# The up projection of a feed-forward as seven products of half blocks, with the weight sums on GpSimd

## The reference

```
h   = h + gate1 * (mixed @ w_out)
hn  = rms_norm(h, norm2_g) * (1 + scale2) + shift2
u   = depthwise_conv_centred(hn @ w_up, conv_w, conv_b)   # w_up: 1024 x 5632, 3 taps along tokens
val, gate = split(u)                                      # 2816 columns each
h   = h + gate2 * ((silu(gate) * val) @ w_down)
```

## Time and profile before

| | |
|---|---|
| median of 3 runs | 1614.38 us (1614.13 to 1614.63) |
| the profiled execution's own time | 1614.99 us |
| its span in the trace | 1613.1 us |
| TensorE busy | 1248.3 us (77%) |
| VectorE busy | 403.0 us (25%) |
| ScalarE busy | 228.1 us (14%) |
| GpSimd busy | 51.8 us (3%) |
| up projection (first to last product) | 228.5 to 384.6 us |

### The profile page before, as it was taken

How to read it: one execution, slowest core, us unless ns; L and a number is a source line. 1 busy time by engine, 2 the same in 40 slices (tenths; PEclk the granted TensorE clock), 3 DMA queues, 4 the chain that set the end, 5 groups by cost and what they waited for, 6 DMA issues and landing times.

```text
span 1613.1 us, 16506 instructions
## 1 busy us (share of the span) xinstructions
PE 1248.3 (77%) x7090; PEld 689.2 (43%) x7090; DVE 403.0 (25%) x817; ACT 228.1 (14%) x447; POOL 51.8 (3%) x77
## 2 busy tenths in 40 slices
PE   7999999999999999998665575666665556565556
PEld 4776578888888889852111111111111111111111
DVE  4667744454033557430000000000000000000001
ACT  2324622222103231120000000000000000000001
POOL 1100000000000031000000000000000000000000
PEclk9999999999999999998887878887888887888788
DMA  9987878667644435589999999999999999999997
GB/s 374 223 230 290 327 255 277 224 235 254 247 150 153 133 108 209 202 341 429 429 428 428 428 428 427 428 428 429 428 429 429 429 428 428 428 428 428 428 428 293
DMA packets 110881, 545.21 MB, mean 338 GB/s; under 512 B 5884, under 2 KB 73468, under 8 KB 80092
## 3 DMA queue, kind: packets, MB, share of 16 engines
q1 hardware_dynamic: 105068, 521.69, 81.6%
q0 software_dynamic: 3328, 18.43, 3.0%
q10 hardware_dynamic: 2416, 4.07, 0.7%
HBM read 539.97 MB, written 4.19 MB: 337 GB/s over the span
## 4 chain that ended last, share of the span: by engine, by line
PE 48%; DMA 41%; DVE 5%; another core or an unknown queue 4%; ACT 1%; issue 1%; SPq 1%; DVEq 0%; ACTq 0%
DMA arena<-in_exp_w_dram 21%; PE L L1658 12%; DMA ring<-in_exp_w_dram 9%; DMA tok<-in_exp_w_dram 9%; PE L L1897 7%; PE X L2116 6%; PE L L1846 5%; PE X L2144 3%; PE X L1824 3%; PE L L2016 2%; PE L L1788 2%; DMA ring<-in_w_ada_dram 2%; PE L L2157 1%; PE X L1946 1%
## 5 line engine op out<-in xcount | busy, mean ns | idle before, releaser
L2116 PE MATMUL X<-arena,side 128*32 128x512 f32 x1280 | 195.4, 741 | 125.3 <-DMA arena<-in_exp_w_dram 125.3
L1658 PE MATMUL L<-tok,ring 128*128 128x256 f32 x960 | 210.1, 380 | 1.2 <-ACT tok L632 0.7
L1658 PEld LDWEIGHTS L<-tok,ring 128*128 128x128 f32 x960 | 181.6, 190 | 32.9 <-issue 8.8
L2116 PEld LDWEIGHTS X<-arena,side 128*32 128x32 f32 x1280 | 39.4, 122 | 272.4 <-DMA arena<-in_exp_w_dram 199.6
L1492 DVE TENSOR_TENSOR side<-side,X 128x512 f32<-128x512 f32 x16 | 11.0, 687 | 502.7 <-ACT side L901 502.7
L2116 PE MATMUL X<-ring,side 128*32 128x512 f32 x512 | 84.3, 790 | 66.7 <-DMA ring<-in_exp_w_dram 66.7
L2144 PE MATMUL X<-ring,side 128*32 128x512 f32 x512 | 82.7, 783 | 27.7 <-DMA ring<-in_exp_w_dram 20.8
L1897 PE MATMUL L<-tok,ring 128*128 128x256 f32 x448 | 99.4, 379 | 0.3 <-ACT tok L753 0.3
L1897 PEld LDWEIGHTS L<-tok,ring 128*128 128x128 f32 x448 | 84.3, 190 | 13.9 <-issue 3.1
L901 ACT ACTIVATE side<-X 128x512 f32<-128x512 f32 x16 | 9.6, 597 | 519.2 <-PE X L2116 519.2
L1497 DVE TENSOR_TENSOR side<-X,side 128x512 f32<-128x512 f32 x16 | 11.1, 691 | 279.1 <-PE X L2144 279.1
(11 more groups left out here) (380 smaller groups left out, 1314.9 us busy)
## 6 DMA issues: line engine op xcount, KB each, us to landing
arena<-in_exp_w_dram SPq DMA_DIRECT2D x96, 2048.0 KB, 50.1
ring<-in_exp_w_dram SPq DMA_DIRECT2D x64, 2048.0 KB, 50.1
ring<-in_w_in_dram SPq DMA_DIRECT2D x34, 1024.0 KB, 5.6
more<-in_exp_w_dram SPq DMA_DIRECT2D x15, 2048.0 KB, 49.5
tok<-in_exp_w_dram SPq DMA_DIRECT2D x15, 2048.0 KB, 49.8
ring<-in_w_ada_dram SPq DMA_DIRECT2D x24, 1024.0 KB, 8.8
ring<-in_w_up_dram SPq DMA_DIRECT2D x22, 1024.0 KB, 7.7
arena<-in_ada_w_dram POOLq DMA_DIRECT2D x15, 1024.0 KB, 7.1
```

The source lines that it names most:

```text
L1658: last = MM(L[:, j % 4, m * T:m * T + T], w[:, k, m * P:m * P + P], src(k), start=(k == 0), stop=(k == KT - 1))
L2116: last = MM(X[CAP * j:CAP * j + CAP, w, :], xe[:, k % 2, k // 2, :], v, start=(k == 0), stop=(k == KT - 1))
```

## The change

With the weight and the tokens of a unit cut in two each way, the four quarters of the result are now made from seven products of sums of quarters (Strassen's scheme, in Winograd's form) in place of eight. A quarter product is four 128x128 weight blocks against 128 tokens, so a unit has 28 products of 128 columns in place of 16 of 256.

GpSimd forms four sums of weight quarters per unit (`up_sums`: each 128 partitions by 4 x 128), three units deep in `upsum`. VectorE forms four sums of `hn` once (`up_inputs`, each 128 by 4 x 128) and adds up quarters in the unit's PSUM bank (`up_top`, `up_right`, `up_corner`). ScalarE copies half a bank to `upkept` (`up_copied`). TensorE's seven products stand in four parts that are spread over three steps of a pipeline.

The sum of `ada_w_2` is cut in halves of 1024 columns, one per unit (`ada_half`). Its loads are issued by GpSimd between the units' sums. The first context unit moves ahead of the last up unit's last part, in two halves, and out from behind the first `w_down` unit; the list `units` moves its load in the same way. `taps` is the former two-tap code, and `first_taps` the former middle tap, as functions.

```diff
+AGAIN = {"up_inputs": ("HF_done", 8), "up_sums": ("filt_summed", 2), "up_sum3": ("qk_rstd", 8),
+         "up_first": ("qk_sum", 8), "up_second": ("w3_done", 8), "up_third": ("scores_done", 16),
+         "up_top": ("qk_inv", 8), "up_right": ("max_ready", 16), "up_corner": ("qk_ready", 8),
+         "up_copied": ("qk_raw", 8)}
...
-        u += [("wup", i), ("wup", FT // 2 + i)] + [("ada2", m) for m in WUP_FILL.get(i, ())]
+        u += [("wup", i)] + ([("cin", CTX_U[0])] if i == FT // 2 - 1 else []) + [("wup", FT // 2 + i)]
+        u += [("ada2", m) for m in WUP_FILL.get(i, ())]
     for i in range(FT // 2):
...
+            eng.wait_ge(S[name], AGAIN[name][1] + n)
+        UPS = [(i, g) for i in range(FT // 2) for g in range(2)]
+        NUP = len(UPS)
+        upin = at(32, 4, 4, P)
+        upsum = (at(24, 4, 4, P), at(42, 4, 4, P), at(50, 4, 4, P))
+        upkept = (at(58, T), at(59, T), at(90, T))
+        uppart = at(91, T)
...
+        def up_weights(n, m, k):
+            i, g = UPS[n]
+            w = slot(upos[("wup", i + g * (FT // 2))]).rearrange("p (k n) -> p k n", k=KT)
+            return w[:, 4 * k:4 * k + 4, m * P:m * P + P]
+        def up_bank(n, m, t):
+            return L[:, pos["wup"][n] % 4, m * T + t * P:m * T + t * P + P]
...
+            def ada_load(j):
                 if j >= 2:
                     pool.wait_ge(S["ada_summed"], j - 1)
-                q, k = m // KT, m % KT
+                q, k = SUMMED[j] // KT, SUMMED[j] % KT
                 pool.dma_start(awide[j % 2], a["ada_w_2"][0, k * P:k * P + P, 2048 * q:2048 * q + 2048]).then_inc(S[f"ada{j % 2}_landed"], 16)
+            def up_sums(n):
+                w, v = upsum[n % 3], lambda m, k: up_weights(n, m, k)
+                up_landed(pool, n)
+                if n >= 3:
+                    again(pool, "up_second", n - 2)
+                G(w[:, 0, :, :], v(1, 0), v(1, 1), ALU.add).then_inc(S["up_sums"], 1)
+                again(pool, "up_sums", 3 * n + 1)
+                G(w[:, 1, :, :], w[:, 0, :, :], v(0, 0), ALU.subtract).then_inc(S["up_sums"], 1)
+                again(pool, "up_sums", 3 * n + 2)
+                G(w[:, 3, :, :], v(0, 1), w[:, 1, :, :], ALU.subtract).then_inc(S["up_sums"], 1)
+                if n >= 3:
+                    again(pool, "up_third", n - 2)
+                G(w[:, 2, :, :], v(0, 0), v(1, 0), ALU.subtract).then_inc(S["up_sum3"], 1)
+            ada_load(0)
+            ada_load(1)
+            pool.wait_ge(S["unit_done"], upos[("wout", 3)] + 1)
+            for n in range(NUP):
+                up_sums(n)
+                if n % 2 == 1 and n >= 5:
+                    ada_load((n - 1) // 2)
+            for j in range(FT // 2, len(SUMMED)):
+                ada_load(j)
...
+            def up_copied(n):
+                again(act, "up_first", n + 1)
+                if n >= 3:
+                    again(act, "up_corner", n - 2)
+                A(upkept[n % 3], L[:, pos["wup"][n] % 4, T:2 * T], ACT.Copy).then_inc(S["up_copied"], 1)
...
+            for s_ in range(NUP + 3):
+                if s_ >= 3:
+                    first_taps(s_ - 3)
+                if s_ == 7:
+                    copy_mod_rows(3)
+                if s_ < NUP:
+                    up_copied(s_)
+                if s_ >= 4 and s_ % 2 == 0:
+                    i = (s_ - 4) // 2
+                    out_of_bank(act, "wup", 2 * i + 1)
...
+            def up_inputs():
+                B = lambda k, t: hn[:, 4 * k:4 * k + 4, t * P:t * P + P]
+                dve.wait_ge(S["norm_ready"], KT + 4)
+                done(V.tensor_tensor(upin[:, 0, :, :], B(0, 1), B(0, 0), ALU.subtract), "up_inputs")
+                dve.wait_ge(S["norm_ready"], 2 * KT)
+                again(dve, "up_inputs", 1)
+                done(V.tensor_tensor(upin[:, 1, :, :], B(1, 1), upin[:, 0, :, :], ALU.subtract), "up_inputs")
+                done(V.tensor_tensor(upin[:, 2, :, :], B(1, 1), B(0, 1), ALU.subtract), "up_inputs")
+                again(dve, "up_inputs", 2)
+                done(V.tensor_tensor(upin[:, 3, :, :], B(1, 0), upin[:, 1, :, :], ALU.subtract), "up_inputs")
+            def up_top(n):
+                again(dve, "up_copied", n + 1)
+                done(V.tensor_tensor(up_bank(n, 0, 0), up_bank(n, 0, 0), upkept[n % 3][:, 0:P], ALU.add), "up_top")
+            def up_right(n):
+                again(dve, "up_second", n + 1)
+                v = uppart[:, (n % 2) * P:(n % 2) * P + P]
+                link(V.tensor_tensor(v, up_bank(n, 1, 0), upkept[n % 3][:, P:T], ALU.add))
+                done(V.tensor_tensor(up_bank(n, 0, 1), up_bank(n, 0, 1), v, ALU.add), "up_right")
+            def up_corner(n):
+                again(dve, "up_third", n + 1)
+                done(V.tensor_tensor(up_bank(n, 1, 1), up_bank(n, 1, 0), upkept[n % 3][:, P:T], ALU.add), "up_corner")
+            def ada_half(j, x):
+                k, c0 = SUMMED[j] % KT, 1024 * x
+                if x == 0:
+                    dve.wait_ge(S[f"ada{j % 2}_landed"], 16 * (j // 2 + 1))
+                    if j:
+                        dve.wait_ge(S["ada_summed"], j)
+                    if k == 0 and j:
+                        dve.wait_ge(S["ada_folded"], 1)
+                c_, v, w = csil2[:, k, 0:1], asum[:, c0:c0 + 1024], awide[j % 2][:, c0:c0 + 1024]
+                if k == 0:
+                    last = V.tensor_scalar(v, w, c_, None, ALU.mult)
+                else:
+                    last = V.scalar_tensor_tensor(v, w, c_, v, ALU.mult, ALU.add)
+                if x == 1:
+                    done(last, "ada_summed")
...
+            def gated(i):
...
+            for s_ in range(NUP + 3):
+                if s_ >= 4:
+                    ada_half((s_ - 4) // 2, s_ % 2)
+                if s_ == 12:
+                    second_mods(0)
+                    reached(dve, "ctx_rstd")
+                if s_ >= 3:
+                    taps(s_ - 3)
+                if s_ < NUP:
+                    up_top(s_)
+                if 2 <= s_ < NUP + 2:
+                    up_corner(s_ - 2)
+                if s_ >= 3 and s_ % 2 == 0:
+                    gated((s_ - 4) // 2)
+                if 1 <= s_ < NUP + 1:
+                    up_right(s_ - 1)
+            ada_half(FT // 2 - 1, 1)
             for j in range(FT // 2, len(SUMMED)):
...
+            def up_input(k, t):
+                return lambda j: h2(4 * k + j)[:, t * P:t * P + P]
+            def up_formed(x):
+                return lambda j: upin[:, x, j, :]
+            def up_first(n):
+                up_landed(pe, n)
+                lin_free(pe, pos["wup"][n])
+                up_product(up_bank(n, 1, 0), up_weights(n, 0, 0), up_input(0, 0), True)
+                up_product(up_bank(n, 0, 0), up_weights(n, 0, 1), up_input(1, 0))
+                again(pe, "up_inputs", 1)
+                again(pe, "up_sums", 3 * n + 1)
+                up_product(up_bank(n, 1, 1), upsum[n % 3][:, 0, :, :], up_formed(0)).then_inc(S["up_first"], 1)
+            def up_second(n):
+                again(pe, "up_top", n + 1)
+                again(pe, "up_inputs", 2)
+                again(pe, "up_sums", 3 * n + 3)
+                up_product(up_bank(n, 1, 0), upsum[n % 3][:, 1, :, :], up_formed(1))
+                up_product(up_bank(n, 0, 1), upsum[n % 3][:, 3, :, :], up_input(1, 1)).then_inc(S["up_second"], 1)
+            def up_third(n):
+                again(pe, "up_right", n + 1)
+                again(pe, "up_inputs", 4)
+                again(pe, "up_sum3", n + 1)
+                up_product(up_bank(n, 1, 0), upsum[n % 3][:, 2, :, :], up_formed(2)).then_inc(S["up_third"], 1)
+            def up_fourth(n):
+                again(pe, "up_corner", n + 1)
+                up_product(up_bank(n, 1, 0), up_weights(n, 1, 1), up_formed(3)).then_inc(S["unit_done"], 1)
...
+            for s_ in range(NUP + 2):
+                if s_ < NUP:
+                    up_first(s_)
+                if s_ >= 2:
+                    up_third(s_ - 2)
+                if s_ == NUP + 1:
+                    ctx_half(0, 1)
+                if 1 <= s_ < NUP + 1:
+                    up_second(s_ - 1)
+                if s_ >= 2:
+                    up_fourth(s_ - 2)
+                if s_ == NUP:
+                    ctx_half(0, 0)
+                if s_ in (3, 5):
+                    mod_products(24 + WUP_FILL[(s_ - 3) // 2][0])
+                if s_ == 10:
+                    mod_columns(3)
+                if s_ == 19:
+                    mod_fold(4)
             def ctx_keys_turned():
```

More of the change, by code:

```diff
@@ L236, in __missing__ @@
                     return self[CHAIN_OF[name]]
+                if name in AGAIN:
+                    return self[AGAIN[name][0]]
                 self[name] = ctx.enter_context(nc.semaphore(name))
@@ new lines, in first_taps @@
+            def first_taps(n):
+                i, g = UPS[n]
+                j = pos["wup"][n]
+                act.wait_ge(S["unit_done"], upos[("wup", i + g * (FT // 2))] + 1)
```

(56 more changed lines are left out.)

30 lines of the change are left out of this document (5 added, 25 removed).

## The result

The changed kernel takes 1616.36 us in the median of 20 runs (1615.34 to 1618.74), the kernel before 1614.19 us beside it. The ratio is 1.0014, 95% interval 1.0007 to 1.002. I had forecast 1609.5 us. The time lies in the range that I gave, but the kernel got slower by 0.14%, where I had forecast a gain of 0.3%; the interval lies above 1, so the small loss is clear of the noise.

The account below looks back on a forecast made before the run. GpSimd was taken to bound the up projection, 6.9 us per unit against TensorE's 6.27. It would end at 386.3 instead of 391.5; with 0.3 lost at the end, 1614.4 - 4.9 = 1609.5 us, range 1602 to 1619.

Parts of the forecast that it names:

- TensorE's saving: Up projection: 1232 short instructions at 0.112 us, 137.9 us, replace 704 taking 153.2 us, saving 15.3 us.
- a kernel bound by TensorE: Rival 1, up projection: TensorE stays the bound, GpSimd under about 6.5 us per unit; gain 13.1, 1601.3 us; chance 0.15.
- rival 4: Expert loads are the path earlier than the windows show, so the saving misses the end: no change; chance 0.05.
- The step that failed: Up projection: VectorE instructions with two SBUF inputs block GpSimd, 29.3 us in all; VectorE falls behind nowhere.
- the sign of being wrong that I had named: Up projection: the forecast is wrong if TensorE waits for VectorE or ScalarE instead of GpSimd's first sums.
- The term at the start: First up unit: third product starts at 231.4 to 232.2 instead of 230.3, waiting for `hn` and `up_inputs`; 1.9 us lost.
- Rival 3: Context pairs: VectorE waits for whole GpSimd sums, `up_corner` comes late, about 1 us a step; 1614 to 1620; chance 0.08.
- Rival 2: Up projection, `up_sums`: GpSimd's queue gaps cost 0.16 each, 13.2 us more in all, so 1622.7 us; chance 0.22.
- the context pairs block GpSimd: Up projection: pairs of context scalings block GpSimd at 0.41 us each, four times, about 2.7 us.
- TensorE's own work would end: End of the up projection: TensorE would finish at 378.7 us if GpSimd's sums were always there.

Follow-up runs that it names:

- the two obstacles removed: Changed kernel with GpSimd held back at the head after unit 0's sums and the context scalings' factor kept in PSUM: 1603.02 us, ratio 0.9932 to the kernel before.
- the gated run: Changed kernel, but GpSimd begins unit 1's sums only after VectorE's four input sums: 1607.4 us, ratio 0.996 to the kernel before.
- short sums: Kernel with head gate and PSUM factor, GpSimd's sums covering 4 of 128 columns from unit 3 on: 1603.59 us, ratio 0.9935 to the kernel before.
- eight sums alone: Kernel before with only eight unused GpSimd sums of 128x512 added beside the scalings of `hn`: 1619.73 us, ratio 1.0035.

## Why the prediction was wrong

**TensorE's saving was nearly right.** An instruction takes 0.112 us. By the chains, 704 instructions took 152.8 us before and 1232 take 138.4 (31.46 / 280 each), so the saving is 14.4 us and not 15.3; I had set the rounded 0.112 against the busy time of the long instructions, which is 0.4 us over their chain. With the two obstacles removed the kernel gains 10.6 us (1613.59 to 1603.02), where I had put 13.1 for a kernel bound by TensorE. `w_down` goes on 9.7 us earlier there, so what is left of the saving at that point reached the end whole, and rival 4 is out.

**The step that failed** is the price of GpSimd and VectorE running side by side. I wrote that a VectorE instruction with two SBUF inputs "stops GpSimd for its duration less 0.2 us", charged 29.3 us of it to GpSimd, and concluded that "VectorE fell behind nowhere in this": VectorE's own wait stood in the sum at nothing. The cost also falls that way, and there it is up to the length of a GpSimd instruction less some 0.3 us: 0.96 and 1.01 in the two kinds of scalings, 0.45 in the mean of `ada_half`, 0.34 in the gate's products. By the groups, GpSimd's 88 sums are busy for 127.0 us against 88 x 1.26 = 111, so it was held for 16 us, about half of what I had charged. VectorE lost about 7.2 us in the scalings of `hn` (10.93 against 3.72 in the gated run), 8.1 in those of the context (8 x 1.01), 8.2 in `ada_half` (31.1 against 22.9 with short sums) and 3.8 in the gate's products (11.3 against 7.5). GpSimd was not the bound: it waited ten times for TensorE or VectorE between 246 and 364 us, while TensorE waited for VectorE's `up_corner`. That is the sign of being wrong that I had named.

The Trainium skill has the rule ("SBUF — State Buffer", Who interferes with whom): whichever engine issues first holds the shared pair of ports for the whole instruction, and the order of issue decides who waits. I gave it and added that by the rule VectorE would wait too, but had no row for that and took the half that I could measure. The rows now agree with it: 1.48 us for a scaling of 0.48 next to a sum of 1.26, so 1.0 added.

**The term at the start** was 1.9 us. The third product started at 239.71 where I had 231.4 to 232.2; against the old kernel's pace (230.3) that is 9.4. I had put line 1216 there as 3.25 us that block GpSimd, and did not ask what blocks line 1216. The lower clock that follows is about 1.6 us more: 160 instructions from 239.71 take 19.62 us against 18.0 at the later pace. The forecast had no term for the clock.

**Rival 3** had the right mechanism and place, VectorE late in the context pairs. I gave it 0.08, and counted up to 0.8 + 1.2 us for the two scalings; they take 2.82 together. Its size of 1 us a step was too high: 14.0 us for two steps against 12.6 is 0.7, and only three of the four pairs lose it. That the time lies in its range of 1614 to 1620 is luck, since most of the loss is in the head, which it did not name.

The sum closes so, up to where `w_down` goes on: 14.4 us saved; 9.4 lost until the third product; 1.6 by the clock; 4.0 in the context pairs, which is what the run with the factor in PSUM gets back between its third product (240.20) and `w_down` (392.57), the clock's share taken off; and 1.1 in small waits that this run has too. That makes -1.7 us, and `w_down` goes on 1.7 us later.

Rival 2 (GpSimd dearer per unit) was wrong: the gaps are small and a sum takes 1.26. Two slips of the working change nothing: by its own rule the context pairs block GpSimd for 2.5 us and not 2.7, and TensorE's own work would end at 378.1 and not 378.7. The main fault of method is this. Work put on an engine that "has room" was checked for its own room, not for what it does to the other engine's shortest instructions on the path.

## What to carry to other kernels

Before giving GpSimd elementwise work, list VectorE's instructions that run beside it and take two tensors from SBUF (here also a `tensor_scalar` of one), and add up to the length of one GpSimd instruction to each, less 0.3 us here. It is worst for many short ones in a row on the path. Two cheap ways out paid here: hold GpSimd back for that stretch (8.7 us), and keep one of the inputs in PSUM (from 1.49 to 0.47 us each, 3.6 us in all). Halving GpSimd's instructions shortened each wait but made GpSimd the bound. An instruction that waits in this way shows as a longer busy time and not as idle time, so compare mean durations with those of the same form elsewhere.

## What the runs showed of the hardware that was not expected

In rows of short instructions the two engines alternate one for one, so eight VectorE instructions of 0.48 us take 1.4 us each beside sums of 1.26, although VectorE's stand back to back in its queue. I had charged the row of eight to GpSimd as one block. Even a VectorE instruction of eight columns with two SBUF inputs (`gain`, at 314.25 us of the changed kernel) took 0.95 us; another of the same form right behind it took 0.15.

The second input in SBUF is not the only case. A `tensor_scalar` of 128x1024 with one tensor from SBUF took 1.24 to 1.81 us beside full sums and 0.74 to 0.75 beside short ones.

TensorE's granted clock was 1.00 from 226 to 232 us and 0.53 in the mean from 232 to 242. Ahead of the fall it had one product of two instructions per 1.4 us. Behind it TensorE was busy without a break from 239.7, at 0.50 until 242.5 and at 1.00 from 244 on. In the gated run, with the eight scalings in 3.72 us, it stayed at 1.00. The lower clock cost 1.6 us in the changed kernel and 2.1 in the run with eight sums alone. So a late engine at the start of a stage can cost more than its own delay.
